# The opening of a decoder layer: x normalised before its transposes, modulation tiles of two chunks summed in two accumulators, one tile in eight summed on TensorE

## What is computed

```python
def rms_norm(x, g):
    y = xf * lax.rsqrt(jnp.mean(xf * xf, axis=-1, keepdims=True) + EPS)
    return (y * g)

def sandwich(x, fn, g_pre, g_post, shift, scale, gate, res_w):
    h = rms_norm(x, g_pre) * (1.0 + scale[:, None]) + shift[:, None]
    y = rms_norm(fn(h), g_post)
    return x + res_w * gate[:, None] * y

cond = jax.nn.silu(c)                       # 2048 numbers
mod = cond @ ada_w[l] + ada_b[l]            # ada_w: 2048 x (9 * 2048)
sh1, sc1, gt1, sh2, sc2, gt2, sh3, sc3, gt3 = jnp.split(mod, N_MOD, axis=-1)
x = sandwich(x, swiglu_1, norm_g[l, 0], norm_g[l, 1], sh1, sc1, gt1, 0.5)
x = sandwich(x, token_mixer, ..., sh2, sc2, gt2, 1.0)
x = sandwich(x, swiglu_2, ..., sh3, sc3, gt3, 0.5)
```

## Time and profile before

| | us |
|---|---|
| median of 3 runs | 1982.17 (1980.71 to 1982.24) |
| profiled execution | 1987.39 |
| its span | 1985.6 |
| mean granted clock | 0.978 |
| TensorE busy (matmul) | 1886.3, 95% |
| VectorE busy | 1412.9, 71% |
| ScalarE busy | 838.1, 42% |

### The profile page before, as it was taken

One profiled execution on the slowest core, in us unless ns is written; L12 is line 12 of the kernel. 1 busy time (PEld: TensorE's weight loads), 2 busy tenths in 40 slices (PEclk: granted clock), 3 DMA queues, 4 the chain that ended last, 5 costly groups with the idle time before them and its releaser, 6 DMA issues.

```text
span 1985.6 us, 21419 instructions
## 1 busy us (share of the span) xinstructions
PE 1886.3 (95%) x8582; PEld 1546.5 (78%) x8582; DVE 1412.9 (71%) x1477; ACT 838.1 (42%) x1067; POOL 20.6 (1%) x25
## 2 busy tenths in 40 slices
PE   2779999999999998999999999999999999999997
PEld 2558888888888888777777787788888888888895
DVE  4987888888888887765765566666666665555556
ACT  2214434443444343374555534644344434443443
POOL 0000000000000000000000000000000000000000
PEclk6779999999999999999999999999999999999999
DMA  9888998999999998545333434566666655555551
GB/s 344 323 318 323 355 347 338 352 340 343 344 342 349 346 344 306 186 141 179 128 127 128 149 135 168 191 233 244 243 233 233 244 201 191 191 191 191 196 196 74
DMA packets 204002, 486.80 MB, mean 245 GB/s; under 512 B 7984, under 2 KB 20992, under 8 KB 188800
## 3 DMA queue, kind: packets, MB, share of 16 engines
q1 hardware_dynamic: 202816, 482.79, 67.1%
q10 hardware_dynamic: 992, 2.63, 0.4%
q0 software_dynamic: 96, 0.02, 0.0%
HBM read 483.31 MB, written 2.10 MB: 244 GB/s over the span
## 4 chain that ended last, share of the span: by engine, by line
PE 86%; DVE 6%; issue 2%; DMA 2%; ACT 1%; DVEq 0%; SPq 0%; POOLq 0%; POOL 0%; ACTq 0%
PE ps_u L1373 10%; PE ps_g L1373 10%; PE ps_u L1374 9%; PE ps_u L1375 9%; PE ps_g L1375 9%; PE ps_g L1374 9%; PE ps_t L1373 4%; PE ps_t L1374 4%; PE ps_t L1375 4%; PE ps_y L1373 4%; PE ps_y L1374 4%; PE ps_y L1375 4%; DVE arena L1136 3%; DMA ada_raw<-in_ada_w 2%; DVE w_lo L842 1%
## 5 line engine op out<-in xcount | busy, mean ns | idle before, releaser
L842 DVE TENSOR_TENSOR w_lo<-w_raw,w_hi 128x1024 fp32r<-128x1024 f32 (+1 forms) x632 | 753.1, 1200 | 458.4 <-ACT w_hi L505 457.2
L505 ACT ACTIVATE w_hi<-w_raw 128x1024 fp32r<-128x1024 f32 (+1 forms) x632 | 657.4, 1042 | 952.1 <-PE ps_u L1375 342.1
L1373 PE MATMUL ps_g<-w_hi,xT_hi 128*128 128x512 f32 (+1 forms) x880 | 347.1, 394 | 21.4 <-DVE w_lo L842 11.4
L1373 PE MATMUL ps_u<-w_hi,xT_hi 128*128 128x512 f32 (+2 forms) x880 | 348.0, 395 | 19.1 <-DVE w_lo L842 18.3
L1375 PE MATMUL ps_g<-w_hi,xT_lo 128*128 128x512 f32 (+1 forms) x880 | 341.8, 388 | 0.0
L1375 PE MATMUL ps_u<-w_hi,xT_lo 128*128 128x512 f32 (+2 forms) x880 | 341.8, 388 | 0.0
L1374 PE MATMUL ps_g<-w_lo,xT_hi 128*128 128x512 f32 (+1 forms) x880 | 341.6, 388 | 0.0
L1374 PE MATMUL ps_u<-w_lo,xT_hi 128*128 128x512 f32 (+2 forms) x880 | 341.5, 388 | 0.0
L866 DVE SCALAR_TENSOR_TENSOR arena<-ada_raw,cond,arena 128x2048 f32<-128x2048 f32 x108 | 253.6, 2348 | 32.7 <-DMA ada_raw<-in_ada_w 32.0
L1373 PEld LDWEIGHTS ps_g<-w_hi,xT_hi 128*128 128x128 f32 x880 | 166.3, 189 | 62.4 <-DVE w_lo L842 19.4
L1373 PEld LDWEIGHTS ps_u<-w_hi,xT_hi 128*128 128x128 f32 x880 | 167.1, 190 | 58.8 <-DVE w_lo L842 22.6
(11 more groups left out here) (239 smaller groups left out, 1542.5 us busy)
## 6 DMA issues: line engine op xcount, KB each, us to landing
w_raw<-in_ffn_w_in SPq DMA_DIRECT2D x160, 1024.0 KB, 4.9
ada_raw<-in_ada_w SPq DMA_DIRECT2D x128, 1024.0 KB, 7.2
w_raw<-in_ffn_w_out SPq DMA_DIRECT2D x80, 1024.0 KB, 5.1
w_raw<-in_mix_w_in SPq DMA_DIRECT2D x32, 1024.0 KB, 5.0
arena<-in_ada_w SPq DMA_DIRECT2D x16, 1024.0 KB, 10.2
w_raw<-in_mix_w_out SPq DMA_DIRECT2D x16, 1024.0 KB, 5.0
w_raw<-in_ffn_w_in SPq DMA_DIRECT2D x16, 768.0 KB, 4.6
w_raw<-in_ffn_w_out SPq DMA_DIRECT2D x8, 768.0 KB, 4.2
```

What stands on the lines that cost most here:

```text
L505: nc.scalar.activation(w_hi[:, u % 4, 0:n, 0:width], w_raw[:, s, 2 * hf:2 * hf + n, 0:width], ACT.Copy).then_inc(hi_done, 1)
L842: nc.vector.tensor_tensor(w_lo[:, u % 4, 0:n, 0:width], w_raw[:, s, 2 * hf:2 * hf + n, 0:width], w_hi[:, u % 4, 0:n, 0:width].bitcast(F32) ...
L1373: nc.tensor.matmul(o, a_hi[:, k, rows], w_hi[:, b, c, 0:width], start=start, stop=False)
```

## The change

It has six parts.

1. x is normalised before it is transposed. ScalarE squares x first, VectorE and POOL make 1/rms early (behind tile 0 of strip 0), ScalarE multiplies x by it into `yacc`, and TensorE transposes that, into eight banks. The diagonal, the spread over the partitions and `rbc` fall away.
2. Each tile now holds two k-chunks (an even and an odd one) of both modulations, 1 MB in two loads of 512 KB. VectorE takes the even chunk with one operation on 2 x 512 columns into `acc`, the odd one with another into a second accumulator (`odd`, in `junk`). `first_sums` adds both in PSUM, with 16 matmuls of one column as before.
3. In strips 1 to 3 tile 0 is summed by TensorE, not by VectorE: `first_raw`, 16 matmuls of one column with `cond` as the moving operand, behind the second unit of the strip before. SyncE's load of tile 4 into the same slot waits for it (`raw_done`). VectorE adds the result in one more small operation.
4. The modulated xT is made by ScalarE alone (scale and shift in place in `xT_raw`, then `xT_hi`), and VectorE only subtracts for `xT_lo`. The order on both is new: the first two units' weights are split first, then xT is made.
5. c is loaded first, x in two loads; the constants of the mixer are loaded by SyncE late in the first SwiGLU, and `negsink` is made at the mixer's start.
6. TensorE has 50 and 40 warm-up matmuls of 128x128 ahead of the transposes and of the first sums.

As in the kernel before, the last two units of a strip stand behind the next strip's column sums.

```diff
+            odd = junk.rearrange("p (s m n) -> p s m n", s=2, m=2)
+            def first_ada(s, i):
+                start = i == (1 if s else 0)
+                dve.wait_ge(ada_landed[i % 4], 32 * (2 * s + i // 4) + 32)
+                for k in range(2):
+                    part = (acc[:, 1:3, s * NB:(s + 1) * NB], odd[:, s % 2, :, :])[k]
+                    raw = first_slots[i % 4].rearrange("p (m k n) -> p m k n", m=2, k=2)[:, :, k, :]
...
+                        ins = nc.vector.scalar_tensor_tensor(part, raw, weight, part, ALU.mult, ALU.add)
...
-            def first_chunks(s):
-                first_cols(s)
-                xt_scale(0, 2 * s)()
-                xt_scale(0, 2 * s + 1)()
-                xt_lo(0, 2 * s)()
+            def strip_start(s):
+                first_columns(s)
+                first_lo(2 * OPENING * s)
+                first_lo(2 * OPENING * s + 1)
+                first_xt_lo(2 * s)
+                first_xt_lo(2 * s + 1)
...
+            for i in range(1, STRIP_TILES):
+                first_ada(0, i)
+            dve.wait_ge(cond_ready, 2)
+            strip_start(0)
             for s in range(STRIPS):
-                for i in range(2 * OPENING):
+                for i in range(2, 2 * OPENING):
                     first_lo(2 * OPENING * s + i)
+                    if s + 1 < STRIPS:
+                        for tile in ((1,), (2, 3), (4, 5), (6, 7))[i - 2]:
+                            first_ada(s + 1, tile)
+                if s + 1 < STRIPS:
+                    strip_start(s + 1)
...
+            def first_xt_hi(b):          # ScalarE
+                act.wait_ge(modcol_done, b // 2 + 1)
+                for c in range(2):
+                    k = 2 * b + c
+                    ins = nc.scalar.activation(xT_raw[:, k, :], xT_raw[:, k, :], ACT.Identity, bias=modcol[:, 0, 1, k:k + 1],
+                                               scale=modcol[:, 0, 0, k:k + 1])
+                link(ins)
+                nc.scalar.activation(xT_hi[:, 2 * b:2 * b + 2, :], xT_raw[:, 2 * b:2 * b + 2, :], ACT.Copy).then_inc(xt_hi_done, 1)
...
             def first_modulation(s):     # SyncE
+                for i in range(STRIP_TILES):
+                    before, j = (s, i - 4) if i >= 4 else (s - 1, i + 4)
+                    if before > 0 and j == 0:
+                        sp.wait_ge(raw_done, before)
+                    elif before >= 0:
+                        sp.wait_ge(ada_done, first_count(before, j))
+                    for m in range(2):
...
+            def first_raw(s):            # TensorE
+                pe.wait_ge(ada_landed[0], 32 * (2 * s + 1))
+                pe.wait_ge(modcol_done, s)
+                for m in range(2):
+                    for c in range(4):
+                        for k in range(2):
+                            ins = nc.tensor.matmul(ps_y[:, 0, 2 * KD + 4 * m + c:2 * KD + 4 * m + c + 1], tile[:, m, k, c * P:(c + 1) * P],
+                                                   cond[:, k:k + 1], start=k == 0, stop=k == 1)
+                ins.then_inc(raw_done, 1)
...
+                        if b == 1 and hf == 0 and s + 1 < STRIPS:
+                            first_raw(s + 1)
                         if b == 2 and hf == 0 and s + 1 < STRIPS:
                             first_sums(s + 1)
```

More of the change, by code:

```diff
@@ L1076, in turn @@
                     xt_rest(b)
[L1078 to L1096, removed]
-                        last = nc.vector.scalar_tensor_tensor(junk[:, (k % 8) * SEQ:(k % 8 + 1) * SEQ], xT,
-                                                              modcol[:, n, 0, k:k + 1], rbc[:, :], ALU.mult, ALU.mult)
-                    last.then_inc(xt_scaled, 1)
-                return f
@@ L1113, in _ @@
-            dve.wait_ge(cond_ready, 1)
-            dve.wait_ge(const_landed, 16 * 4)
-            dve.wait_ge(ident_landed, 16)
-            nc.vector.tensor_scalar(negsink[:, :], sink[:, :], -1.0, None, ALU.mult)
-            def first_ada(s, kg):
-                before = chain[0]
-                for i in range(8):
-                    k, m = divmod(i, 2)
-                    count = 8 * s + 2 * kg + m
-                    slot = (2 * kg + m) % 4
-                    if k == 0:
-                        dve.wait_ge(ada_landed[slot], 16 * (count // 4) + 16)
-                        if kg:
-                            dve.wait_ge(ada_done, count - 1)
-                    else:
-                        dve.wait_ge(dve_chain, before + i - 1)
-                    part = acc[:, MODS_PRE[m][1], s * NB:(s + 1) * NB]
-                    raw, weight = first_slots[slot][:, k * NB:(k + 1) * NB], cond[:, 4 * kg + k:4 * kg + k + 1]
-                    if kg == 0 and k == 0:
+            evens = [0]
@@ new lines, in _ @@
+            odd = junk.rearrange("p (s m n) -> p s m n", s=2, m=2)
[5 more added lines that the diff above has]
+                    raw = first_slots[i % 4].rearrange("p (m k n) -> p m k n", m=2, k=2)[:, :, k, :]
+                    weight = cond[:, 2 * i + k:2 * i + k + 1]
+                    if start:
@@ L1448, in gate_rows @@
                 ins.then_inc(gbc_done, 1)
-            def row_scale(n):
-                pe.wait_ge(diag_ready, n + 1)
-                for t in range(TILES):
-                    ins = nc.tensor.matmul(ps_y[:, 1, t * P:(t + 1) * P], ones[:, :], diag[:, t, :], start=True, stop=True)
-                ins.then_inc(rb_done, 1)
-                pe.wait_ge(rb_copied, n + 1)
             def warm(n, ps):
@@ new lines, in _ @@
+            nc.tensor.transpose(ps_y[:, 1, 0:KD], mod_rows[:, :], ident[0:KD, 0:KD]).then_inc(cond_raw, 1)
+            pe.wait_ge(c_landed, 16 * 6)
+            nc.tensor.transpose(ps_y[:, 0, 0:7 * KD], small_rows[:, :], ident[0:7 * KD, 0:7 * KD])
+            nc.tensor.transpose(ps_y[:, 0, 7 * KD:9 * KD], more_rows[:, :], ident[0:2 * KD, 0:2 * KD]).then_inc(small_done, 1)
+            warm(50, ps_g)
+            pe.wait_ge(cond_ready, 2)
+            for t in range(TILES):
+                pe.wait_ge(xn_first, t + 1)
+                for k in range(KD):
+                    ins = nc.tensor.transpose(banks[k // 2][:, (k % 2) * SEQ + t * P:(k % 2) * SEQ + (t + 1) * P],
+                                              yacc[:, t, k * P:(k + 1) * P], ident[:, :])
+                    if t == 1 and k % 2:
+                        ins.then_inc(xt_done, 1)
@@ L1579, in first_sums @@
                 ins.then_inc(cols_done, 1)
+            warm(40, ps_g)
             first_sums(0)
```

172 lines of the change are left out of this document (70 added, 102 removed).

## The result

The changed kernel takes 2004.24 us (median of 4 runs, 2002.95 to 2005.56), the kernel before in the same rounds 1982.20 (1980.71 to 1983.76): a ratio of 1.0108, 95% interval 1.0096 to 1.0121, so 22 us slower. Forecast were 1975.4 and a range of 1967 to 1981.5. The forecast was wrong, in its sign too.

The account below looks back on a forecast made before the run. TensorE, busy 95% of the span, was taken as the bound, VectorE in the opening's strips. Strip 1's sums 7.7 us earlier, then two rounds of 34.65 against 34.2, left 6.8: 1982.17 - 6.8 = 1975.4 us; range 1967 to 1981.5.

Parts of the forecast that it names:

- the ring: Strips 1 to 3: tile 4's load waits for TensorE's tile-0 pass, behind column sums needing tile 7; 34.65 us a round.
- column sums: In the ring: TensorE's one-column matmuls that sum the accumulators, at the lower clock level (1.2 GHz), 3.6 us.
- lead-in: Opening up to strip 0's first unit: that unit starts at 41.0 us against 51.95, 10.9 us less.
- pass over tile 0: In the ring: TensorE's 16 one-column matmuls for tile 0, priced at the upper clock level (2.4 GHz), 2.03 us.
- first tile into an idle queue: In the ring: issue 0.6 and landing 4.8 us for the first tile, 5.4 us.
- three more tiles and VectorE's work on them: In the ring: three further tiles, 8.1 us, then two VectorE operations and its start, 2.5 us.
- VectorE's work: In a strip: VectorE needs 25.7 us in all, so it bounds nothing.
- Carry-over: Behind the opening: the 6.8 us gained there reach the end one for one, as TensorE bounds the stage behind.
- half-size loads: Rival, tile loads in front of VectorE: they do not run on each other's heels; 13 us slower, 1995; chance 0.06.
- (2): Rival, opening: TensorE keeps the upper clock level, 31.0 us a round, 1966 us in all; chance 0.16.
- (3): Rival: worse clock in the ring's units and tile-0 pass adds 4 us a round; 1983, no gain; chance 0.12.
- The slower side: Whole kernel: slower by more than some 4 us, from half-size loads and the edge of (3); chance 0.08.

## Why the prediction was wrong

**The step that failed** is the price of TensorE's one-column matmuls in the sum of the ring ("column sums at the lower level ... 3.6" and "16 matmuls of one column for tile 0: 2.03") and in the lead-in (2.03 for the sums). The rows were read rightly as times and wrongly as counts: `x16` was taken for 16 matmuls and was 8. The listing gave the true number, two loops of two and four.

The forecast's own terms, beside what the trace of the changed kernel shows for the round from the first column sum of strip 1 to that of strip 2 (74.29 to 114.28; us):

| term | forecast | measured |
|---|---|---|
| column sums | 3.6 | 6.85 |
| four units | 13.05 | 13.03 |
| pass over tile 0 | 2.03 | 3.66 |
| first tile into an idle queue | 5.4 | 5.01 |
| three more tiles and VectorE's work on them | 10.6 | 11.44 |
| round | 34.65 | 39.99 |

Two terms are off by more than 1 us, and both are the count of matmuls. The three strips took 38.57, 39.99 and 41.89 us, forecast 33.0, 34.65 and 34.65. Against 34.2 a strip that is a loss where the forecast had a tie. The last scales came 23.4 us behind the forecast's 139.8 (163.19). Of these the sums make 12 (2.4 in the lead-in, 3.25 in each strip), the passes 5 and the warm-ups 3; some 3.5 are left, 1.5 of them the slow load of the last ring. In its own terms:

- **Lead-in**: first unit at 46.20, forecast 41.0, before 51.95. Tiles, norm and transposes were as forecast or earlier (VectorE through with the tiles at 34.4, forecast 35.5). Then the 40 warm-ups, priced without a row as ending at 33, ran 9.17 us to 38.34, and the sums took 4.4 instead of 2.03: 16 at the upper level are 3.63, and the level fell before their end, 2.9 us into them, although nothing stood between them and the warm-ups. The scales are at 42.74 for 37.5.
- **VectorE's work**: right. An operation of 128x1024 takes 1.24 us (2.48 for two), forecast 1.20; busy 24.7 us a strip, forecast 25.7.
- **The ring**: right as a mechanism. SyncE waits 50.8 us for L1540, TensorE idles 9.3 us before the sums (forecast about 10), tile 4 comes into an idle queue 5.0 us behind its release (forecast 5.4). Moving the pass in front of two units takes 15 us off.
- **The last ring** took 41.9 us, 2 more than the one before. Its first tile was usable 6.9 us behind its issue instead of 5.0 (138.25 to 145.14). Why that load was slower is open.
- **Carry-over**: near one for one, not exactly. Behind the last scales nothing changes up to the transposes (31.93 and 31.91 us). From the last scales to the end of the span the thirteen profiles of this case take 1836.8 to 1843.4 us (the two of the kernel before 1839.0 and 1836.8, the changed one 1840.0). What makes this spread of 6.6 us is open, so a gain at the last scales of one profile tells the gain of the whole to a few us only.
- **The rivals**: the half-size loads run on each other's heels. So the rule of at least 1 MiB a load (the Trainium skill, DMA: Bandwidth & Descriptors, "Rules for kernel authors") is not borne out for queued halves of 512 KB: 1 MB in 2.71 us either way. The fixed 2.0 us that the prediction takes from there stand in the Trainium skill as a fit for loads issued from GpSimd; these were issued by SyncE. TensorE did not keep the upper level (2), the level at the sums was the forecast one. (3) named the right places, sums, pass and units, but as a matter of clock, not of count. Its price was too low even in its own terms: two more units at 5.1 for 2.75 are 4.7 and the pass 1.5, some 6 us a round, where the forecast has 4. The slower side was given 0.08. The tile-0 pass did have bounds, 2.03 to 3.57, but both were rows of 8 matmuls, so a wrong count passed through both.

What removes the loss agrees with this: half of the sums -11 us, no ring -12, a shorter ring -15. They don't add up, because sums and ring lie on one loop; with the sums halved, the pass early and the clock kept up at the sums the strip falls to 31.8 us, 2 above the transfers' pace.

## What to carry to other kernels

Before a row of a trace is used as a price, divide its count by the number of instructions in the listing: the trace counts records, and one instruction can leave one or two, by the type of its operands. A bound read from the same row does not guard against this. When an engine takes over a buffer's last use, write down the loop that its slot release closes, with every piece on it, and move the release to the front of that engine's work first: here that was worth 15 us, more than halving the sums. Warm-ups paid here only where they ended close ahead of the work and did not delay it: 5 us for the 20 that ended 1.9 us ahead of the sums, nothing for the 20 that ended 7 us ahead, and next to nothing for the 40 that the sums had to wait for. Read a mean share of the DMA engines against a stretch without gaps before calling it full: 0.98 still held a gap of 2.5 us.

## What the runs showed of the hardware

- Matmuls on plain float32 operands leave two records each (16 are `x32`, 40 are `x80`), those on float32r operands one (twelve a unit). 8 float32 matmuls of one column, each with its own 128x128 weights, take 3.57 us at the lower level and 1.95 at the upper; 16 take 6.85 to 6.99 and 3.63. Being only one column wide did not make them cheap: 0.43 us each at the lower level.
- 20 warm-ups of 128x128 (4.63 us) that ended 1.87 us ahead of the sums: upper level; 7.06 us ahead: lower, as behind 6.3 us of idle without any. 34 of them (7.75 us) that ended 2.91 and 3.54 us ahead: the sums began at the upper; 3.99 us ahead: lower.
- The level also fell without any idle time, in or right behind a row of one-column matmuls: 2.9 us into the first sums right behind 9.17 us of warm-ups, and in the unit right behind the pass of 3.63 us (matmuls of 0.63 us from 58.25 and from 99.14, where 0.39 is the upper level's).
- Loads of 512 KB, queued, bring 1 MB in 2.71 us, as loads of 1 MB do; the first into an idle queue is usable after 5.0 us, once after 6.9. A stretch without a gap moves 387 GB/s and reads as a share of 1.05.
